# Sums of squares by two fp32r products with high and low parts, and q's and k's reciprocal roots one block later

## What is computed

```python
def rmsnorm(x, g):
    return x * lax.rsqrt(jnp.mean(x * x, axis=-1, keepdims=True) + NORM_EPS) * g

h = rmsnorm(x, norm_mix)
proj = h @ w_in                      # z, xbc, dt, q, k, v, q_idx, k_idx, w_idx, sc_b, sc_c, sc_h
q = rmsnorm(q.reshape(bsz, t, 8, 64), q_norm)      # per head of 64
k = rmsnorm(k.reshape(bsz, t, 8, 64), k_norm)
# q and k feed attention over the top 128 causal keys that an indexer picks
y = y.reshape(bsz, t, D_SSD) * silu(z)
y = rmsnorm(y.reshape(bsz, t, 2, 512), norm_g)     # the gated norm, per group of 512
x = x + concat([y_ssd, y_att, y_sc]) @ w_out
x = x + (silu(conv3(h2 @ w_gate)) * (h2 @ w_up)) @ w_down
```

## Time and profile before

| | us |
|---|---|
| median of 3 runs | 2115.19 (2113.59 to 2116.62) |
| the profiled execution | 2107.81 |
| its span | 2105.9 |
| TensorE busy | 2097.7 |
| VectorE busy | 1571.6 |
| GpSimd busy | 1276.8 |
| ScalarE busy | 1008.8 |

### The profile page before, as it was taken

How to read it: one execution, slowest core, us unless ns; L and a number is a source line. 1 busy time by engine, 2 the same in 40 slices (tenths; PEclk the granted TensorE clock), 3 DMA queues, 4 the chain that set the end, 5 groups by cost and what they waited for, 6 DMA issues and landing times.

```text
span 2105.9 us, 34272 instructions
## 1 busy us (share of the span) xinstructions
PE 2097.7 (100%) x11280; PEld 1771.7 (84%) x11280; DVE 1571.6 (75%) x2805; ACT 1008.8 (48%) x1468; POOL 1276.8 (61%) x732
## 2 busy tenths in 40 slices
PE   9999999999999999999999999999999999999999
PEld 7777777887888888888888888888888888888888
DVE  6589565557663226888888888888788799988987
ACT  6343334344433446555546545555555554444443
POOL 5345334444454656676767767767767676666665
PEclk9999999999999999999999999999999999999999
DMA  6224123333333444354454544544544766655744
GB/s 211 85 74 126 61 70 99 97 101 103 102 102 123 146 142 145 121 180 135 159 164 134 167 157 140 173 155 144 170 144 146 245 223 199 226 187 186 237 152 132
DMA packets 150119, 308.75 MB, mean 147 GB/s; under 512 B 13272, under 2 KB 54424, under 8 KB 149880
## 3 DMA queue, kind: packets, MB, share of 16 engines
q1 hardware_dynamic: 103568, 250.39, 36.3%
q10 hardware_dynamic: 46440, 56.94, 8.7%
HBM read 261.64 MB, written 45.51 MB: 146 GB/s over the span
## 4 chain that ended last, share of the span: by engine, by line
PE 92%; DVE 6%; issue 1%; DMA 1%; ACT 0%; SPq 0%; ACTq 0%; DVEq 0%
PE ps L879 40%; PE ps L878 21%; PE ps L687 10%; PE ps L691 9%; PE ps L688 9%; DVE work L1467 1%; DVE work L1466 1%; DVE work L1370 1%; DVE work L1369 1%; PE ps L785 1%; PE ps L771 1%; PE ps L757 0%; DVE work L1458 0%; DVE work L1445 0%; PE ps L826 0%
## 5 line engine op out<-in xcount | busy, mean ns | idle before, releaser
L879 PE MATMUL ps<-comb,fhi 128*128 128x512 f32 x3507 | 1228.6, 392 | 0.0
L878 PE MATMUL ps<-comb,flo 128*128 128x256 f32 x3507 | 985.2, 281 | 0.1
L879 PEld LDWEIGHTS ps<-comb,fhi 128*128 128x128 f32 x3507 | 656.5, 187 | 143.9
L631 POOL TENSOR_TENSOR flo<-raw,fhi 128x1024 fp32r<-128x1024 f32 (+2 forms) x252 | 484.9, 1935 | 356.8 <-ACT fhi L1217 356.3
L878 PEld LDWEIGHTS ps<-comb,flo 128*128 128x128 f32 x3507 | 662.4, 189 | 7.4 <-DVE ps L1834 2.9
L601 POOL TENSOR_TENSOR wlo<-raw,whi 128x512 fp32r<-128x512 f32 x260 | 361.7, 1405 | 394.2 <-ACT whi L997 343.3
L631 POOL TENSOR_TENSOR flo<-sum,fhi 128x1024 fp32r<-128x1024 f32 (+2 forms) x168 | 324.2, 1935 | 37.7 <-ACT fhi L1217 37.4
L1217 ACT ACTIVATE fhi<-ps 128x1024 fp32r<-128x1024 f32 (+2 forms) x168 | 141.8, 844 | 419.9 <-DVE ps L1708 215.0
L687 PE MATMUL ps<-hhi,whi 128*128 128x512 f32 x784 | 317.3, 405 | 0.6 <-ACT hhi L1146 0.6
L691 PE MATMUL ps<-hlo,whi 128*128 128x512 f32 x784 | 306.6, 391 | 0.1
L688 PE MATMUL ps<-hhi,wlo 128*128 128x512 f32 x784 | 305.7, 390 | 0.0
(11 more groups left out here) (248 smaller groups left out, 2644.2 us busy)
## 6 DMA issues: line engine op xcount, KB each, us to landing
raw<-w_gu SPq DMA_DIRECT2D x176, 512.0 KB, 3.8
raw<-w_in SPq DMA_DIRECT2D x196, 256.0 KB, 3.2
raw<-w_dn SPq DMA_DIRECT2D x96, 256.0 KB, 2.8
raw<-w_dn SPq DMA_DIRECT2D x64, 320.0 KB, 3.1
act_hi<-pair_sums ACTq DMA_DIRECT2D x20, 896.0 KB, 4.2
act_lo<-pair_sums ACTq DMA_DIRECT2D x20, 896.0 KB, 8.3
raw<-w_out SPq DMA_DIRECT2D x64, 256.0 KB, 3.3
comb<-act_hi SPq DMA_DIRECT2D x21, 512.0 KB, 4.0
```

Of the source, the lines that this page charges most:

```text
L631: nc.gpsimd.tensor_tensor(flo[s][:, 0:w], src[:, 0:w], fhi[s][:, 0:w].bitcast(F32), ALU.subtract).then_inc(f_lo_pool, 1)
L878: nc.tensor.matmul(dst[:, 0:HT], flo[s][:, w], both[:, HI, :], start=fresh and k == 0, stop=False, skip_group_check=True)
L879: ins = nc.tensor.matmul(dst, fhi[s][:, w], both, start=False, stop=k == n - 1, skip_group_check=True)
```

## The change

- The float32 product of each sum of squares becomes two fp32r products accumulated in the same bank: 0/1 matrix by high part, 0/1 matrix by low part. GpSimd makes an fp32r copy `sums` of the two matrices once.
- For q and k, ScalarE squares twice: into `nsq` (float32) and into `nhi` (fp32r). GpSimd makes `nlo = nsq - nhi` right after the low part of quarter 4(7+m), ahead of the next weight's. For this GpSimd's loop over quarters 24 to 63 is unrolled.
- TensorE's two products stand at `side(6+m, 3)`, a quarter later than the product before. ScalarE's `rsqrt` stands at `side(7+m, 0)`, again one quarter later and ahead of the next square, instead of `side(6+m, 3)`. VectorE's Newton step stays where it was.
- For the gated norm VectorE makes `ghi` and `glo` after the last sum of each group, and `y_done` is raised after them.

```diff
+            def low_square(m):
+                pool.wait_ge(nq_sq, 2 * m + 1)
+                nc.gpsimd.tensor_tensor(nlo[:, m % 2, :], nsq[:, m % 2, :], nhi[:, m % 2, :].bitcast(F32), ALU.subtract).then_inc(nq_sq, 1)
...
+            for n in range(8 * NQ0, 8 * NQ1):
+                low(n % 8, n, T)
+                m = n // 4 - 2 - TILE_OF["q", 0]
+                if n % 4 == 0 and 0 <= m < 8:
+                    low_square(m)
...
-                if kind in ("q", "k") and q == 2:
+                if kind in ("q", "k") and q == 3:
                     m = j + (4 if kind == "k" else 0)
-                    pe.wait_ge(nq_sq, m + 1)
+                    pe.wait_ge(nq_sq, 2 * m + 2)
...
-                    nc.tensor.matmul(bank(4 + m % 2), C("halves"), nsq[:, m % 2, :], start=True, stop=True).then_inc(nq_sum, 1)
+                    nc.tensor.matmul(bank(4 + m % 2), exact("halves"), nhi[:, m % 2, :], start=True, stop=False)
+                    nc.tensor.matmul(bank(4 + m % 2), exact("halves"), nlo[:, m % 2, :], start=False, stop=True).then_inc(nq_sum, 1)
...
-                        nc.tensor.matmul(bank(7), C("ones"), gsum, start=True, stop=True).then_inc(gn_sum, 1)
+                        nc.tensor.matmul(bank(7), exact("ones"), ghi[:, :], start=True, stop=False)
+                        nc.tensor.matmul(bank(7), exact("ones"), glo[:, :], start=False, stop=True).then_inc(gn_sum, 1)
...
+                if kind2 in ("q", "k") and q == 0:
+                    m = j2 + (4 if kind2 == "k" else 0)
+                    sc.wait_ge(nq_sum, m + 1)
+                    if m:
+                        sc.wait_ge(nq_done, m)
+                    rsqrt(nrs, bank(4 + m % 2), 1.0 / 64, nq_r0)
...
-                    A(nsq[:, m % 2, :], qkT[:, m, :], ACT.Square).then_inc(nq_sq, 1)
+                    if m:
+                        sc.wait_ge(nq_sq, 2 * m)
+                    A(nsq[:, m % 2, :], qkT[:, m, :], ACT.Square)
+                    A(nhi[:, m % 2, :], qkT[:, m, :], ACT.Square).then_inc(nq_sq, 1)
...
-                if kind in ("q", "k") and q == 3:
-                    m = j + (4 if kind == "k" else 0)
-                    sc.wait_ge(nq_sum, m + 1)
-                    if m:
-                        sc.wait_ge(nq_done, m)
-                    rsqrt(nrs, bank(4 + m % 2), 1.0 / 64, nq_r0)
...
+                                ch_.link(V.tensor_tensor(gsum, gsum, gtmp, ALU.add))
+                                ch_.link(V.tensor_copy(ghi[:, :], gsum))
+                                V.tensor_tensor(glo[:, :], gsum, ghi[:, :].bitcast(F32), ALU.subtract).then_inc(y_done, 1)
```

More of the change, by code:

```diff
@@ L124 @@
 ATT_AT = 4 * 17
+NQ0 = (TILE_OF["q", 0] + 2) // 2
+NQ1 = (TILE_OF["k", 3] + 3) // 2 + 1
 SPLIT_AT = 4 * 46
@@ L239, in hybrid_block, with exact @@
         x2d = at(yq(6, 1), "x2d", [P, 2, T])
-        ctx.enter_context(nc.sbuf_tensor("reserved", [P, (EXTRA + 16 * KB) // 4], F32))
+        nhi = at(20 * KB, "nhi", [P, 2, T], F32R)
+        nlo = at(24 * KB, "nlo", [P, 2, T], F32R)
+        ghi = at(EXTRA, "ghi", [P, T], F32R)
+        glo = at(EXTRA + 2 * KB, "glo", [P, T], F32R)
+        sums = at(EXTRA + 16 * KB, "sums", [P, 2, P], F32R)
+        ctx.enter_context(nc.sbuf_tensor("reserved", [P, (EXTRA + 17 * KB) // 4], F32))
         def C(name):
             return cm[:, CM_NAMES.index(name), :]
+        def exact(name):
+            return sums[:, ("ones", "halves").index(name), :]
         def par(name, j=0, n=1):
@@ L602, in low @@
                                         whi[:, slot % NW, 0:width].bitcast(F32), ALU.subtract).then_inc(lo_ready, 1)
-            with pool.Fori(0, (QN_OUT - 4) // 8) as i:
+            def low_square(m):
+                pool.wait_ge(nq_sq, 2 * m + 1)
+                nc.gpsimd.tensor_tensor(nlo[:, m % 2, :], nsq[:, m % 2, :], nhi[:, m % 2, :].bitcast(F32), ALU.subtract).then_inc(nq_sq, 1)
+            with pool.Fori(0, NQ0) as i:
+                for q in range(8):
+                    low(q, 8 * i + q, T)
+            pool.wait_ge(const_loaded, 16 * 3)
+            nc.gpsimd.tensor_copy(sums[:, :, :], cm[:, 3:5, :])
+            for n in range(8 * NQ0, 8 * NQ1):
[3 more added lines that the diff above has]
+                    low_square(m)
+            with pool.Fori(NQ1, (QN_OUT - 4) // 8) as i:
                 for q in range(8):
@@ L1008, in side @@
                 kind, j, _ = TILES[t - 1] if 0 < t <= NPROJ else ("", 0, 0)
+                kind2, j2 = TILES[t - 2][:2] if 2 <= t <= NPROJ + 1 else ("", 0)
+                if kind2 in ("q", "k") and q == 0:
[4 more added lines that the diff above has]
+                    rsqrt(nrs, bank(4 + m % 2), 1.0 / 64, nq_r0)
                 if kind in ("q", "k") and q == 0:
@@ L1582, in side @@
                             ch_.link(V.tensor_tensor(gtmp, y, y, ALU.mult))
-                            V.tensor_tensor(gsum, gsum, gtmp, ALU.add).then_inc(y_done, 1)
+                            if j2 % 4 < 3:
+                                V.tensor_tensor(gsum, gsum, gtmp, ALU.add).then_inc(y_done, 1)
+                            else:
+                                ch_.link(V.tensor_tensor(gsum, gsum, gtmp, ALU.add))
+                                ch_.link(V.tensor_copy(ghi[:, :], gsum))
+                                V.tensor_tensor(glo[:, :], gsum, ghi[:, :].bitcast(F32), ALU.subtract).then_inc(y_done, 1)
                     if (t, q) in ((37, 1), (45, 1)):
```

## The result

The changed kernel takes 2118.67 us (median of 22 runs, 2116.60 to 2121.53) against 2115.43 for the kernel before on the same chip (22 runs). The ratio is 1.0020, 95% interval 1.0010 to 1.0029: slower by 2 to 6 us. It was timed twice more beside later experiments: 1.0012 (0.9998 to 1.0026) and 1.0020 (1.0009 to 1.0032). The forecast was 2115.5 with +0.3 us for the change. The time lies in its range, but near its upper end: the change costs 3 us or so where next to nothing was forecast.

What follows compares the result with a forecast made beforehand. TensorE was taken as the bound, held at v1's transposes by VectorE's unbroken chain. +0.7 there, 0 and -0.4 for the gated norms gave +0.3 us: 2115.2 to 2115.5 us, range 2110.3 to 2118.9.

Steps and rivals of the forecast that it cites:

- What bounds the kernel: Whole kernel: TensorE, busy throughout with 92% of the chain, but without slack against VectorE's unbroken chain at v1's transposes.
- Step (a): Start of VectorE's chain: ReLU 1.3 us sooner against a second square of 0.63 us, together -0.7 us.
- rival 2: VectorE, 114.8 to 202.4 us: GpSimd's longer burst hits everything it can; slower, middle +5 us, 2120; chance 0.10.
- Step (b): VectorE's Newton steps colliding with GpSimd's longer bursts: L1445 +1.8 us and L1369 +0.8 us.
- Step (c): VectorE's chain: the lone fourth `low` goes, freeing both L1470 instructions, -1.2 us.
- Sum: VectorE's chain up to v1's transposes: +0.7 us, in place of the -3.3 us that q's and k's products save.
- The waits for `nlo`: TensorE at `side(6+m, 3)`: waits of 1 to 2 us for m = 4 to 7, nothing on top.
- Gated norms: First gated norm: 0, its saving lost at L812's wait for VectorE; second: -0.4 us.
- 1 (full savings): TensorE's savings show in full as VectorE's chain shortens by 4 us: 2110.4, or 2110.8; chance 0.15.
- 3: VectorE's chain shortens in part, its start gaining the whole 2.56 us: -2.5 us in the middle, 2112.7; chance 0.20.
- The signs it named: Profile after: paired products, waits about 3 us, no VectorE idle time from 114 to 202 us, bursts of five, L1445 1.66, L1470 near 0.4.
- From profile to time: Whole kernel: the profiled execution, 7.4 us below the runs' median, goes from 2107.8 to 2108.1; the difference is carried over.

Runs made afterwards that it cites:

- after_psum: Changed kernel with q's and k's Newton steps and scaling working in the sums' PSUM bank; ratio 0.9997 to the kernel before.
- half_after: Changed kernel with every second top-k round left out; ratio 0.9972 to the kernel before.
- no_nlo: Changed kernel without GpSimd's `nlo`, the second product taking `nhi` again; ratio 1.0018 to the kernel before.
- ctl_after: The changed kernel once more, unchanged; ratio 1.0012 to the kernel before.
- products_only: Changed kernel with the two q and k products and `rsqrt` back at their old quarters; ratio 1.0009 to the kernel before.
- gated_only: Kernel before with only the gated norm's products made fp32r; ratio 0.9998 to the kernel before.
- order_only: Kernel before with q's and k's float32 product and `rsqrt` one quarter later; ratio 1.0019, timed again 1.0002.

## Why the prediction was wrong

- **What bounds the kernel: right.** TensorE met VectorE's unbroken chain at v1, and the products' 0.41 us each didn't reach the end there. after_psum and half_after show both halves: the chain holds 4 us back, and they come once it has idle time.
- **Step (a), the start of VectorE's chain: this is the step that failed.** Forecast -0.7, measured +2.5 us. Its two terms were sized well enough (ReLU sooner: -1.3 forecast, -1.0 measured; second square: +0.63 forecast, +0.51; together -0.5 in no_nlo). But the step went through ScalarE alone. GpSimd's `nlo` for m = 1 and 2 lies on pairs of L1458, which read SBUF twice, and the delay travels by ScalarE's ReLU and high part to a second pair. The mechanism was known and stood in rival 2, with the right instructions (L1458) and a fair price for each (0.75 to 1.66; measured up to 1.6). It was put down as unlikely on the ground that "most collisions are there already". That is true of the Newton steps and false of L1458: in the trace of the kernel before all 21 of them are free (0.48 to 0.75 us by their width; four of them are in the earlier trace rows), and what is free has the most to lose.
- **Step (b), collisions of the Newton steps:** L1445 right (1.8 forecast and measured, 1.66 each). L1369 forecast +0.8, measured -0.1: one (m = 1) was hit as forecast, but m = 7 came free. no_nlo, where the same term is +2.0, shows that such terms turn on tenths of a microsecond of position.
- **Step (c), both L1470 free:** forecast -1.2, measured -1.4.
- **Sum:** +0.7 forecast, +2.8 measured at v1. The steps other than (a) were forecast at +1.4 and came to +0.3. That +0.3 is partly luck: m = 7's L1369 is free in two of the kernel's three executions, but hit in ctl_after, where v1 comes at 206.1.
- **The waits for `nlo`:** forecast 1 to 2 us for m = 4 to 7, measured four of 0.5 to 1.5. They cost nothing on top, as said. products_only shows what they'd be at the old place: up to 2.7 us.
- **Gated norms:** right, 0 and -0.48.
- **Rivals.** 1 (full savings) didn't happen, but is what after_psum gives. 2 happened in its kind and about half its size; its price "from 4.6 us on" was too far away, as it needed everything to be hit. 3 didn't.
- **The signs it named** came true but for VectorE, which waits until 115.86 where no idle time was forecast from 114 on: pairs 0.23 us apart, waits of 3.9 us at m = 4 to 7 and v1 (3 forecast), bursts of five, L1445 at 1.66, both L1470 free. That the time still lay in the range is the range's width: its upper end stood for L1369 hit every time, which isn't what happened.
- **From profile to time.** The prediction took a profile 7.4 us below the median and carried the difference over. That was sound as far as the profiles tell: the executions differ by that much in the MLP.

By the Trainium skill, page "SBUF — State Buffer", section "Who interferes with whom", VectorE's instruction with two SBUF inputs and GpSimd's SBUF reads exclude each other. The runs here agree: 0.70 us with one operand in PSUM, 1.66 with both in SBUF, under the same bursts. The prediction priced that rule at up to 1 us for each new `nlo` and set it aside for the smaller sum from rows; for the `nlo` that met free instructions the rule had the better price.

## What to carry to other kernels

When an engine's new operation excludes another's, don't ask how much already collides, but list what is free now and lies where the new operation will land; on a chain without idle time each such instruction counts in full, while ahead of an idle time it costs nothing (the pair at 81.62). Before giving TensorE less to do, look at the first place where it waits for another engine's unbroken chain, and shorten that chain first: here an operand moved to PSUM turned a start of the MLP 2 to 3 us late into one 5 us early, and 6.6 with the gated norm's, too. For effects of 0.1 to 0.2% compare a landmark ahead of the part that varies (here the MLP's start), counted from one ahead of the change, and don't take one timing of ten runs as the last word.

## What the hardware showed besides

**TensorE has two paces at one granted clock.** Pairs of the MLP's products in gated_only, at about 920 and 1078 us of the same execution, with clock 1.00 in both and no wait:

```profile
919.98 0.40 PE L903 MATMUL ps<-comb,fhi 128*128 128x512 f32 x1
...
921.75 0.40 PE L903 MATMUL ps<-comb,fhi 128*128 128x512 f32 x1
```

```profile
1078.12 0.39 PE L903 MATMUL ps<-comb,fhi 128*128 128x512 f32 x1
...
1079.85 0.39 PE L903 MATMUL ps<-comb,fhi 128*128 128x512 f32 x1
```

Five pairs take 1.77 us in the one stretch and 1.73 in the other. The 800 us from 860 on hold 4592 and 4590 products in the two profiles of the kernel before, 4550 in gated_only, 4549 and 4567 in the two of order_only's program, 4564, 4564 and 4585 in the three of the changed kernel's. From the MLP's first product to the end the executions take 1295 to 1308 us, and those of one program differ by up to 7 us (order_only's: 1307.5 and 1300.7), a good part of what single runs differ by. What sets the pace isn't known: the granted clock is 1.00 and TensorE is busy for the whole of these 800 us in all of them.

**GpSimd is slowed too.** `nlo` and `low` for one quarter take 1.27 to 1.30 us each alone. In the bursts beside VectorE's two-SBUF instructions four `low` take 6.38 us in the kernel after, and 5.05 in after_psum, where VectorE reads PSUM.
